# State-space input matrices built in turned form, with powers and coefficients read on GpSimd's own queue

## The reference

```python
lam = lax.complex(a_re, a_im)
dt = jnp.exp(log_dt)[..., None]
a_bar = jnp.exp(lam * dt)
b_mat = lax.complex(b_re, b_im)
b_bar = ((a_bar - 1.0) / lam)[..., None] * b_mat
c_mat = lax.complex(c_re, c_im)

def scan_dir(u_row, r, reverse):
    bu = jnp.einsum('sgh,gph->sgp', u_row, b_bar[r])
    a = jnp.broadcast_to(a_bar[r], bu.shape)
    _, states = lax.associative_scan(_ssm_combine, (a, bu), reverse=reverse, axis=0)
    return jnp.einsum('sgp,ghp->sgh', states, c_mat[r]).real
```

## Time and profile before

| | us |
|---|---|
| median of 3 runs | 1870.55 (1868.81 to 1870.89) |
| profiled execution | 1867.82, span 1866.0 |
| TensorE busy | 1786.5 (96%) |
| VectorE busy | 1300.6 (70%) |
| ScalarE busy | 778.5 (42%) |
| GpSimd busy | 47.9 (3%) |
| matmuls L561 (128 transposes) | start 343.1 to 647.5 |

### The profile page before, as it was taken

The page is one execution under the profiler, slowest core; times in us unless marked ns, Lnnn a source line. Parts: engine busy times, 40 slices in busy tenths (PEclk is TensorE's granted clock), DMA queues, the critical chain, the costliest instruction groups (busy, mean ns, idle before and its releaser), DMA issues.

```text
span 1866.0 us, 25467 instructions
## 1 busy us (share of the span) xinstructions
PE 1786.5 (96%) x9314; PEld 1438.1 (77%) x9314; DVE 1300.6 (70%) x2397; ACT 778.5 (42%) x1271; POOL 47.9 (3%) x39
## 2 busy tenths in 40 slices
PE   7999999999999992999999999999999999999998
PEld 6886688888888862888888788779755788888886
DVE  5868967767886669536655686458899976776465
ACT  5237944422342372424321342244687343333211
POOL 0000000000000000000000000000043100000000
PEclk9999999999999995999999999999999999999999
DMA  7320022444555489434444676224101223223532
GB/s 213 104 89 23 1 71 98 145 149 149 172 156 154 141 255 139 147 102 136 147 147 146 202 231 228 80 68 125 36 33 46 68 83 106 94 90 101 180 102 68
DMA packets 99928, 224.98 MB, mean 121 GB/s; under 512 B 19297, under 2 KB 48609, under 8 KB 99825
## 3 DMA queue, kind: packets, MB, share of 16 engines
q1 hardware_dynamic: 53520, 166.81, 29.2%
q10 hardware_dynamic: 46304, 56.77, 9.8%
HBM read 202.68 MB, written 20.87 MB: 120 GB/s over the span
## 4 chain that ended last, share of the span: by engine, by line
PE 90%; DVE 4%; SPq 2%; DMA 1%; ACT 1%; issue 1%; ACTq 0%; DVEq 0%
PE PS L444 26%; PE PS L446 26%; PE PS L445 26%; PE PS L637 2%; SPq L408 2%; PE PS L1024 1%; PE PS L662 1%; PE PS L998 1%; DMA Tm<-k_scratch 1%; PE PS L650 1%; PE PS L1032 1%; PE PS L561 1%; PE PS L818 1%; PE PS L504 1%; PE PS L1025 1%
## 5 line engine op out<-in xcount | busy, mean ns | idle before, releaser
L1657 DVE TENSOR_TENSOR WL<-raw,WH 128x1024 fp32r<-128x1024 f32 x228 | 279.6, 1231 | 275.0 <-ACT WH L1120 265.7
L1120 ACT CAST WH<-raw 128x1024 fp32r<-128x1024 f32 x228 | 237.3, 1046 | 489.0 <-PE PS L446 409.9
L444 PE MATMUL PS<-XH,WH 128*128 128x512 f32 x928 | 366.3, 395 | 4.5 <-issue 4.3
L446 PE MATMUL PS<-XH,WL 128*128 128x512 f32 x928 | 362.8, 391 | 0.0
L445 PE MATMUL PS<-XL,WH 128*128 128x512 f32 x928 | 362.6, 391 | 0.0
L444 PE MATMUL PS<-WH,AH 128*128 128x512 f32 x688 | 269.6, 392 | 0.0
L446 PE MATMUL PS<-WH,AL 128*128 128x512 f32 x688 | 267.9, 389 | 0.0
L445 PE MATMUL PS<-WL,AH 128*128 128x512 f32 x688 | 267.7, 389 | 0.0
L444 PEld LDWEIGHTS PS<-XH,WH 128*128 128x128 f32 x928 | 175.0, 189 | 42.9 <-issue 7.2
L444 PE MATMUL PS<-WH,XH 128*128 128x512 f32 (+2 forms) x512 | 197.3, 385 | 11.1 <-DVE XL L1728 10.4
L446 PEld LDWEIGHTS PS<-XH,WL 128*128 128x128 f32 x928 | 175.1, 189 | 37.2
(11 more groups left out here) (368 smaller groups left out, 2462.2 us busy)
## 6 DMA issues: line engine op xcount, KB each, us to landing
raw<-units_dram SPq DMA_DIRECT2D x272, 512.0 KB, 3.3
ada_late<-ada_units_dram ACTq DMA_DIRECT2D x48, 512.0 KB, 3.8
wi_scratch<-WIe ACTq DMA_DIRECT2D x16, 512.0 KB, 2.9
ca_scratch<-CAr ACTq DMA_DIRECT2D x32, 256.0 KB, 3.5
WI<-wi_scratch SPq DMA_DIRECT2D x16, 512.0 KB, 8.3
CA<-ca_scratch SPq DMA_DIRECT2D x16, 512.0 KB, 7.3
Tm<-k_scratch SPq DMA_DIRECT2D x8, 512.0 KB, 20.3
bc<-bc_dram ACTq DMA_DIRECT2D x16, 160.0 KB, 2.2
```

Of the source, the lines that this page charges most:

```text
L444: pe.matmul(o, lh, rh, start=start, stop=False)
L446: return pe.matmul(o, ll, rh, start=False, stop=stop)
L1120: nc.scalar.copy(WH[:, (u + n) % SLOTS], raw[:, s]).then_inc(hi_done, 1)
L1657: v.tensor_tensor(WL[:, s], raw[:, (u + n) % 2], WH[:, s].bitcast(F32), ALU.subtract).then_inc(unit_ready, 1)
```

## The change

The input matrices are built with the chunk's inputs on the partitions from the outset.

- Once, behind tile 5, TensorE transposes the powers PWI (eight transposes, `powers_turned`), ScalarE copies them to WIe and stores them to a new scratch `p_dram` (`evict_powers`). For this the output powers move from tile 4 to tile 3; the last of them raises the semaphore that TensorE waits for (PWI was written before it, and WIe shares its place with their scratch pd).
- Per block GpSimd's queue issues two loads of 512 KB: the block's powers, each row to 16 partitions (PT), and the coefficients b, turned on the host, each row to 8 groups of partitions (BT). It starts them when VectorE's sums of the block before are done, since PT and BT have one buffer.
- VectorE multiplies them with the gain as a per-partition scalar in eight instructions of 128x256 (DpT), and two sums write WIe. `bc` is still scaled by the gain, for the small matmuls.
- The 16 groups of transposes behind the turns and their 16 copies are gone; ScalarE stores WIe behind tile T - 1 (`store_wi`).
- One more small load (gain_t) on ScalarE's queue with the other parameters. Waits on semaphores are renumbered to fit.

```diff
@@ -168,8 +168,11 @@
         pd = at("pd", 16 * KB, [P, 4, CHUNK + 1, NG])
-        WIp = at("WIp", 16 * KB, [P, 2, BG, CHUNK, SG])
-        WIe = at("WIe", 20 * KB, [P, 2 * BG * P])
+        PT = at("PT", S0, [P, BG, 2, P])
+        BT = at("BT", 16 * KB, [P, BG, 2, P])
+        DpT = at("DpT", S0 + 9 * KB, [P, 2, BG, 2, P])
+        WIe = at("WIe", 20 * KB, [P, BG, 2, P])
+        gain_t = at("gain_t", small + 5888, [P, NG])
         Ke = at("Ke", 24 * KB, [P, 2, LAGS, SG])
...
@@ -426,6 +431,13 @@
+                pool.wait_ge(wi_stored, 32)
+                pairs = lambda x: x[:, :, :, :].rearrange("p g r q -> p (g r q)")
+                sh = [CHUNK, SG, 2 * BG * P]
+                for b in range(NB):
+                    pool.wait_ge(w_done, 2 * b + 1)
+                    nc.gpsimd.dma_start(pairs(PT), p_dram[:, BG * b:BG * (b + 1)].rearrange("j g r q -> j (g r q)").unsqueeze(1).to_broadcast(sh)).then_inc(pb_in, 16)
+                    nc.gpsimd.dma_start(pairs(BT), io["bt"][b].unsqueeze(0).to_broadcast(sh)).then_inc(pb_in, 16)
                 pool.wait_ge(cv_v, 4)
...
@@ -547,24 +559,21 @@
-                def matrices(b):
+                def powers_turned():
+                    pe.wait_ge(w_done, 1)
+                    for j in range(CHUNK):
+                        m = pe.transpose(PS[:, 4 + j // 4, (j % 4) * P:(j % 4 + 1) * P], PWI[:, j].rearrange("p r g -> p (r g)"), ident[:, :])
+                    m.then_inc(m_turned, 1)
+                def kernels(b):
                     k = TURNS[b]
-                    pe.wait_ge(w_done, 2 * b + 2)
+                    pe.wait_ge(ca_done, 2 * b + 2)
                     if k // 8 % 4 == 2:
                         pe.wait_ge(down_add, 8 * (k // 32) + 4)
-                    if b:
-                        pe.wait_ge(ev_wi, b)
-                    for n in range(2 * BG):
-                        m = pe.transpose(PS[:, bank0(k) + n // 4, (n % 4) * P:(n % 4 + 1) * P],
-                                         WIp[:, n % 2, n // 2].rearrange("p j h -> p (j h)"), ident[:, :])
-                    m.then_inc(m_turned, 1)
-                def kernels(b):
-                    pe.wait_ge(ca_done, 2 * b + 2)
                     if b:
...
@@ -690,8 +699,8 @@
                                 late_rows(1)
-                        elif k in TURNS:
-                            matrices(TURNS.index(k))
+                        elif k == 5:
+                            powers_turned()
                         elif k - 1 in TURNS:
...
@@ -1151,15 +1160,19 @@
-                def evict_wi(b):
-                    bank = 0 if TURNS[b] // 8 % 4 == 2 else 4
-                    a.wait_ge(m_turned, b + 1)
-                    if b:
-                        a.wait_ge(wi_stored, 16 * b)
-                    nc.scalar.copy(WIe[:, :], PS[:, bank:bank + 2, :].rearrange("p a n -> p (a n)")).then_inc(ev_wi, 1)
-                    a.wait_ge(ev_wi, b + 1)
-                    a.dma_start(wi_dram[b], WIe[:, :]).then_inc(wi_stored, 16)
+                def evict_powers():
+                    a.wait_ge(m_turned, 1)
+                    nc.scalar.copy(WIe[:, :, :, :].rearrange("p g r q -> p (g r q)"), PS[:, 4:6, :].rearrange("p a n -> p (a n)")).then_inc(ev_wi, 1)
+                    a.wait_ge(ev_wi, 1)
+                    for r in range(2):
+                        a.dma_start(p_dram[:, :, r, :].rearrange("j g q -> g j q"),
+                                    WIe[64 * r:64 * r + 64].rearrange("g a r q -> g (a r) q")).then_inc(wi_stored, 16)
+                def store_wi(b):
+                    a.wait_ge(w_done, 2 * b + 3)
+                    a.dma_start(wi_dram[b], WIe[:, :, :, :].rearrange("p g r q -> p (g r q)")).then_inc(wi_stored, 16)
...
@@ -1315,8 +1329,10 @@
                             bc_load(TURNS.index(k + 4))
-                        if k in TURNS:
-                            evict_wi(TURNS.index(k))
+                        if k == 5:
+                            evict_powers()
+                        if k + 1 in TURNS:
+                            store_wi(TURNS.index(k + 1))
                         if k - 1 in TURNS:
...
@@ -1827,27 +1843,30 @@
                         order.after(v.tensor_tensor(PC[0:64, :, ri, :], pd[0:64, 2 * ri], pd[0:64, 2 * ri + 1], op))
-                        order.after(v.tensor_tensor(PC[64:P, :, ri, :][:, ::-1], pd[64:P, 2 * ri], pd[64:P, 2 * ri + 1], op))
+                        m = v.tensor_tensor(PC[64:P, :, ri, :][:, ::-1], pd[64:P, 2 * ri], pd[64:P, 2 * ri + 1], op)
+                        if ri == 0:
+                            order.after(m)
+                            order.wait()
+                    m.then_inc(w_done, 1)
                     order.wait()
+                    v.wait_ge(w_done, 1)
-                    gs = slice(b * BG, (b + 1) * BG)
-                    sh = [P, BG, CHUNK, SG]
-                    x = [PWI[:, :, ri, gs].rearrange("p m g -> p g m").unsqueeze(3).to_broadcast(sh) for ri in range(2)]
-                    y = [bc[:, b % 2, ri].unsqueeze(2).to_broadcast(sh) for ri in range(2)]
                     v.wait_ge(bc_in[b % 2], 16 * (b // 2 + 1))
                     step(v.tensor_tensor(bc[:, b % 2, 0:2], bc[:, b % 2, 0:2], bc[:, b % 2, 4:5].to_broadcast([P, 2, BG, SG]), ALU.mult))
-                    for n, (i, j) in enumerate(((0, 0), (1, 1), (0, 1), (1, 0))):
-                        v.tensor_tensor(Dp[:, n, :, 0:CHUNK], x[i], y[j], ALU.mult).then_inc(d_prod, 1)
-                    if b:
-                        v.wait_ge(m_turned, b)
-                    v.wait_ge(d_prod, 8 * b + 2)
-                    v.tensor_tensor(WIp[:, 0], Dp[:, 0, :, 0:CHUNK], Dp[:, 1, :, 0:CHUNK], ALU.subtract).then_inc(w_done, 1)
-                    v.wait_ge(d_prod, 8 * b + 4)
-                    v.tensor_tensor(WIp[:, 1], Dp[:, 2, :, 0:CHUNK], Dp[:, 3, :, 0:CHUNK], ALU.add).then_inc(w_done, 1)
+                    v.wait_ge(pb_in, pb_in_base + 32 * b + 32)
+                    for n in range(2):
+                        for g in range(BG):
+                            y = BT[:, g] if n == 0 else BT[:, g, ::-1]
+                            v.scalar_tensor_tensor(out=DpT[:, n, g], in0=PT[:, g], scalar=gain_t[:, BG * b + g:BG * b + g + 1], in1=y,
+                                                   op0=ALU.mult, op1=ALU.mult).then_inc(d_prod, 1)
+                    v.wait_ge(wi_stored, 32 + 16 * b)
+                    for n, op in enumerate((ALU.subtract, ALU.add)):
+                        v.wait_ge(d_prod, 12 * b + 4 + 4 * n)
+                        v.tensor_tensor(WIe[:, :, n], DpT[:, n, :, 0], DpT[:, n, :, 1], op).then_inc(w_done, 1)
...
@@ -1855,15 +1874,15 @@
                     y = [bc[:, b % 2, 2 + ri].unsqueeze(2).to_broadcast(sh) for ri in range(2)]
-                    v.wait_ge(w_done, 2 * b + 2)
+                    v.wait_ge(w_done, 2 * b + 3)
                     for n, (i, j) in enumerate(((0, 0), (1, 1), (0, 1), (1, 0))):
                         v.wait_ge(ca_stored, 32 * b)
-                    v.wait_ge(d_prod, 8 * b + 6)
+                    v.wait_ge(d_prod, 12 * b + 10)
                     v.tensor_tensor(CAr[:, 0], Dp[:, 0], Dp[:, 1], ALU.subtract).then_inc(ca_done, 1)
-                    v.wait_ge(d_prod, 8 * b + 8)
+                    v.wait_ge(d_prod, 12 * b + 12)
                     v.scalar_tensor_tensor(out=CAr[:, 1], in0=Dp[:, 2], scalar=-1.0, in1=Dp[:, 3], op0=ALU.mult, op1=ALU.subtract).then_inc(ca_done, 1)
...
@@ -2055,7 +2074,7 @@
                             input_powers()
-                        if k == 4:
+                        if k == 3:
                             output_powers()
```

More of the change, by code:

```diff
@@ L84 @@
 INPUTS = ("x_in x_t units ada_units c_cols ident rope_cos rope_sin rope2_cos rope2_sin norm_mix_col norm_ffn_col "
-          "q_gain k_gain lam_vecs subln_col a_re a_im log_dt bc d_col d_gain lag_mask "
+          "q_gain k_gain lam_vecs subln_col a_re a_im log_dt bc bt gain_t d_col d_gain lag_mask "
           "b_ada_col b_ada_row ctx conv_w conv_b conv_ln_g conv_ln_b q_norm_col kv_norm_col b_o ln1_g ln1_b "
@@ L259, in program @@
         wi_dram = nc.dram_tensor("wi_scratch", [NB, P, 2 * BG * P], F32).ap()
+        p_dram = nc.dram_tensor("p_scratch", [CHUNK, NG, 2, P], F32).ap()
         ca_dram = nc.dram_tensor("ca_scratch", [NB, P, 2 * BG * P], F32).ap()
@@ L323, in program @@
         m_turned, k_done, ev_wi, ev_k, k_mid = (sem(n) for n in ("m_turned", "k_done", "ev_wi", "ev_k", "k_mid"))
+        pb_in, pb_in_base = sem("pb_in"), 0
         wi_stored, ca_stored, k_stored = sem("wi_stored"), sem("ca_stored"), [sem(f"k_stored{i}") for i in range(2)]
@@ L395, in _ @@
                 sp.wait_ge(k_done, NB)
-                sp.wait_ge(wi_stored, 16 * NB)
+                sp.wait_ge(wi_stored, 32 + 16 * NB)
                 sp.wait_ge(ca_stored, 32 * NB)
@@ L580, in evacuated @@
                 def evacuated(b):
-                    pe.wait_ge(ev_wi, b)
```

(10 more changed lines are left out.)

## The result

The changed kernel is slower, by 1.2%: 1893.51 us (median of 4 runs, 1889.35 to 1895.2) against 1870.1 (1868.81 to 1870.89); the ratio is 1.0119, with an interval of 1.0104 to 1.0134. Forecast were 1863.5 and a range of 1859 to 1869. The profiled execution has a time of 1895.19 and a span of 1893.4 us, 27.4 more than before.

The account below looks back on a forecast made before the run. TensorE was taken to bound the first MLP. Terms -14.3 + 0.9 + 3.4 + 0.8 + 1.7 + 0.4 = -7.1 us gave 1860.7 for the profiled execution, 1863.5 at the median's level; range 1859 to 1869.

Parts of the forecast that it names:

- the new transfers: GpSimd's pair of 512 KB loads per block: 7.6 us to landing, hidden except at block 7, +0.4 us.
- Transposes removed: Sixteen groups of eight transposes leave TensorE's queue, -14.3 us; eight transposes of the powers are added, +0.9 us.
- The total: All terms of the whole kernel sum to -7.1 us, giving 1863.5 us.
- The wait at tile 5: TensorE stands behind tile 5 until VectorE's output powers are done, +3.4 us, bounds 0 and 4.
- The clock: Behind the tile 5 wait TensorE may run at half speed, costing 1.7 us or nothing; half taken, +0.8 us.
- VectorE's block: Per block, eight products take 3.2 us instead of four in 2.4, +0.8 us of VectorE.
- Tile 32: TensorE's wait for the additions behind block 7 grows by 1.7 us, plus 0.4 for the pair landing late.
- The regular blocks: TensorE's matmuls with CAr had 3.71 us to spare; 2.0 remain, so nothing is lost.
- The rest: One more parameter load, the WIe stores and their buffer's reuse on ScalarE's queue: 0, the load at most +0.5 us.
- Rival A: VectorE holds up GpSimd's transfer starts; pair 12.6 us, tile 32 waits 5.4: 1868.5 us, no change; chance 0.13 with similar pairs.
- Rival B: Transfers become the bound, VectorE waiting before products in ten blocks; at 16 us per pair +15, 1886 us; chance 0.09.
- Rivals C and D: C: VectorE becomes the bound, -5.5 us, 1865, inside the forecast's 0.75. D: TensorE's queue isn't shortened; held excluded, no chance given.

Follow-up runs that it names:

- e1: The changed kernel with both loads of the pair cut to 64 KB from the second block on; 1863.86 us, ratio 0.9968 to the kernel before.
- e7: The changed kernel with TensorE waiting at tile 5 for the input powers alone; 1888.85 us, ratio 1.0107 to the kernel before.
- e6: The changed kernel with both loads reading 128 distinct 4 KB rows of the weights, same bytes and target; 1866.96 us, ratio 0.998 to the kernel before.
- e17: The changed kernel with both loads reading 16 starts 256 bytes apart, each 8 times, in a 16 by 8 pattern; 1869.11 us, ratio 0.9991.
- e9: The changed kernel with each partition given two pieces of 2 KB from two places; 1866.58 us, ratio interval 0.9963 to 0.9984.
- e14: The changed kernel with distinct source rows, each load of the pair issued as two of 2 KB per partition; 1865.2 us, ratio 0.9975.
- e18: The changed kernel with a coefficient row per partition, two copies of the powers, and TensorE waiting at tile 5 for input powers alone; 1869.8 us, ratio 0.9996.
- e3: The changed kernel with both loads of the pair issued from ScalarE's queue instead of GpSimd's; 1908.47 us, ratio 1.0202 to the kernel before.
- e16: The changed kernel with a coefficient row per partition, two copies of the powers, tile 5 waiting for input powers alone, and moved turns; 1872.51 us, ratio 1.0013.

## Why the prediction was wrong

The step that failed is in the part on the new transfers: "I take 7.6, nearest to the row of those issued together", and "In total 17 MB more move in the stretch, and the DMA engines were half idle". Two things were wrong in it. The rows I took the price from are transfers with 128 rows outermost, and I carried it to a pattern of 8 by 16 without asking whether that spreads alike; the two took 10.4 and 11.0 us, and the pair 11 to 12 instead of the 7.6 that I took. And I priced the pair only by who waits for the pair. Its main victims are the weight loads beside it: at tile 32 one landed after 10.9 us, although the mean share of the DMA engines before was only 0.50. I asked only what the pair's landing would delay, which is 11.4 us of VectorE's time in two places, and not what it would delay of other traffic, which is 109.6 us of ScalarE's. In the sum the pair stood at +0.4; with the pair cut to 64 KB (e1) the MLP ends 26.4 us earlier than in the changed kernel.

Point by point. **Transposes removed** (-14.3 + 0.9): it fits. In e1 the stretch is 3.2 us shorter than before (it begins 0.3 us later and ends 2.8 us earlier); its waits are 3.2 us at tile 5, 3.8 for the first `CAr` and 1.9 at tile 32, and with up to 1.7 us for the one stretch at half clock that leaves 12.1 to 13.8 us, against 13.4 in the sum. **The total**: that e1's median of 1863.86 us meets the forecast of 1863.5 is in part luck. The sum has no term for the first `CAr`, and in e1's profile the stretch gained 3.2 us and not 7.1; the profiled execution is only 0.9 us faster than the one before, and the rest of the 6 us between the medians isn't found in it. **The wait at tile 5** (3.4): measured 3.13, from VectorE's PC as said. **The clock** (0.8 as half of 1.7): here it did dip, and eight transposes took 1.97 us; behind the same wait in e1 it did not, and they took 1.09:

```profile
324.29 1.97 PE L566 MATMUL PS<-ident,PWI 128*128 128x128 f32 x8 [3.13 <-DVE PC L1846]
...
325.01 1.09 PE L568 MATMUL PS<-ident,PWI 128*128 128x128 f32 x8 [3.20 <-DVE PC L1848]
```

The second row is e1's (its L568 is the same line). So the half that I took was a fair price. e7 took the wait and the dip away. **VectorE's block** (eight products in 3.2 us): the row at 487.71 has eight in 3.26. **Tile 32** (1.7 + 0.4): with the shape cured 3.0 us (e6); in the changed kernel 11.9, since I had priced no late weight load. **The regular blocks** (nothing): six waits for `CAr` of up to 3.6 us, with the pair cut only the first block's, 3.8, which I had priced at nothing too. **The rest** (0): one more parameter load gave 0.63 us more idle before the read at 241.67 (2.43 against the earlier trace rows), and the MLP began no later.

Rival A (descriptors wait for VectorE): not seen; in e6, with the same issues and VectorE busy for 287.6 us of the 380 instead of 269.9, the two landed in 5.4 and 6.5 us. Rival B came out in its sign and, by chance, nearly in its price, 1886 against 1893.5, but by another path: not VectorE's wait for BT in ten blocks (two waits, 11.4 us) but ScalarE's for weights. Its argument for, 16 partitions reading the same 4 KB, isn't the cause either, as e17 shows. That I gave it 0.09 because "the DMA engines are half idle" is the same error once more. Rivals C and D: not seen.

What stays open: `Tm` is waited for between 31.8 us (e9) and 39.8 (after) in these kernels (before 35.9, e1 32.8, e6 39.6, e14 34.5), so the 3.9 us at that place are no mark of the change, and I didn't find what sets them. Differences of a few us between two kernels can come from there; the end of the MLP (before 669.24, after 692.79, e1 666.40, e6 665.56, e17 668.49, e18 669.11) is free of it. That a transfer with a pattern of 8 outermost also has one extra packet of 4 bytes per row on GpSimd's queue (4,608 small ones instead of 512) was seen in each such kernel. They are not needed for the loss: in e3 ScalarE's queue has the same 8 by 16 pattern with only 256 small ones for its 32 transfers (51,856 packets in all, 47,504 in the changed kernel, 4,096 of the difference being data), and it is slower still. In the changed kernel they last 13 ns each in the mean; whether they lengthen the packets beside them was not tried apart.

## What to carry to other kernels

Before a transfer is priced by a row of the trace, compare the outermost dimension of both patterns: 8 outermost (here a broadcast) made each load of the pair take 10 to 11 us instead of 5 to 8, and the median weight load of another queue 5.3 us instead of 3.6, at the worst place 10.9. If the shape can't be had directly, a second copy in DRAM gives 16 by 8 (e16, e18). A half-idle mean of the DMA engines is no cover for a load that ScalarE and VectorE take in order: ask which loads may come late beside the new ones, and what stands behind them in those engines' queues.

## What the hardware showed that I had not expected

- The same pair from ScalarE's queue cost 15 us more than from GpSimd's (1908.5 against 1893.5), with 11 packets at once for both instead of 15 to 20.
- One transfer at a time was far slower than both together (1939.9 us): each alone had only 8 to 11 packets under way, and they took 8.4 + 9.4 us one behind the other.
- 128 partitions reading almost one place in DRAM cost little: 6.5 and 8.3 us to landing in e17 against 5.4 and 6.5 from distinct rows.
- Waits of TensorE of 3.13 and 2.84 us amid full work were each followed by a lower granted clock, 0.83 in the 10 us around each. But the length of the wait doesn't decide it: behind the 3.20 us at the same place in e1 the clock stayed at 1.00.
